# Sample rows taken eighth of nine in the output projection, and router logits from rows that are normalised only at the logits

## The reference

```python
def token_mixer(x, ...):
    z = rmsnorm(x, norm1_g) @ w_in           # q, kv, u, v, two gates
    attn = ...                               # latent attention, prompt or paged cache
    u = gelu(z_u); v = rmsnorm(gelu(z_v), sgu_norm_g)
    sgu = u * spatial_gate(v, w_s, b_s)      # mixes rows of one 128-row chunk
    merged = sigmoid(z_ga) * attn + sigmoid(z_gb) * sgu
    return x + merged @ w_o

def channel_mixer(x, ...):
    xt = rmsnorm(x, norm2_g)                 # x * rsqrt(mean(x*x) + eps) * norm2_g
    g_logit = xt @ w_rg + b_rg               # 8 groups, the best one is taken
    e_logit = xt @ w_re + b_re               # 64 experts, the best two of that group
    y = grouped_expert_ffn(xt, expert, weights, w_gate, w_up, w_down)
    return x + y
```

## Time and profile before

| | us |
|---|---|
| median of 3 runs | 2028.76 |
| lowest and highest run | 2025.43, 2029.05 |
| span of the profiled execution (first to last instruction) | 2028.6 |
| PE busy | 1864.8 (92%) |
| DVE busy | 600.3 (30%) |
| ACT busy | 426.1 (21%) |
| POOL busy | 300.7 (15%) |

### The profile page before, as it was taken

The page is one execution under the profiler, slowest core; times in us unless marked ns, Lnnn a source line. Parts: engine busy times, 40 slices in busy tenths (PEclk is TensorE's granted clock), DMA queues, the critical chain, the costliest instruction groups (busy, mean ns, idle before and its releaser), DMA issues. The chain is left out here.

```text
span 2028.6 us, 26767 instructions
## 1 busy us (share of the span) xinstructions
PE 1864.8 (92%) x10622; PEld 1093.4 (54%) x10622; DVE 600.3 (30%) x1385; ACT 426.1 (21%) x904; POOL 300.7 (15%) x428
## 2 busy tenths in 40 slices
PE   7999999999999999998999997999498888988884
PEld 5644444444445656565666664565365555655551
DVE  3110000022203334334455554565313211111116
ACT  3211111100003223322334443222111001110103
POOL 1021221111100000000111112244412111111100
PEclk9999999999999999988999998999599899998997
DMA  7212211378820000023999996344599999999986
GB/s 232 106 68 79 74 42 64 121 264 273 290 70 1 1 1 1 1 62 106 277 298 298 300 298 255 146 180 158 201 376 420 420 417 417 413 404 403 407 353 259
DMA packets 105267, 433.86 MB, mean 214 GB/s; under 512 B 24208, under 2 KB 29808, under 8 KB 74384
## 3 DMA queue, kind: packets, MB, share of 16 engines
q1 hardware_dynamic: 84880, 331.06, 43.3%
q0 software_dynamic: 20160, 101.24, 15.2%
q10 hardware_dynamic: 128, 0.20, 0.0%
HBM read 389.22 MB, written 63.66 MB: 223 GB/s over the span
## 5 line engine op out<-in xcount | busy, mean ns | idle before, releaser
L851 PE MATMUL psum<-arena 128*128 128x512 f32 (+1 forms) x1280 | 527.5, 567 | 0.0
L851 PEld LDWEIGHTS psum<-arena 128*128 128x128 f32 x1280 | 239.7, 190 | 259.9 <-issue 236.0
L1286 PE MATMUL psum<-arena 128*64 128x256 f32 (+1 forms) x2048 | 283.4, 410 | 64.6 <-DMA arena<-in_w_up_dram 64.5
L1286 PEld LDWEIGHTS psum<-arena 128*64 128x64 f32 (+1 forms) x2048 | 204.4, 155 | 133.8 <-issue 77.8
L1305 PE MATMUL psum<-arena 128*64 128x512 f32 (+1 forms) x512 | 131.5, 595 | 1.5 <-DVE arena L2243 0.9
L1916 DVE COPY arena<-psum 128x512 f32<-128x512 f32 (+5 forms) x52 | 27.8, 545 | 348.0 <-PE psum L896 194.0
L1046 PEld LDWEIGHTS psum<-arena 128*128 128x128 f32 x1024 | 112.7, 141 | 30.3 <-issue 27.4
L1046 PE MATMUL psum<-arena 128*128 128x128 f32 x1024 | 126.6, 276 | 1.2 <-DVE arena L1970 1.2
L1455 ACT ACTIVATE arena<-psum 128x512 f32<-128x512 f32 (+1 forms) x72 | 40.4, 562 | 411.5 <-PE psum L851 398.6
L1176 PE MATMUL psum<-arena 128*128 128x512 f32 x256 | 114.7, 606 | 1.3 <-ACT arena L1504 1.3
L2239 DVE TENSOR_TENSOR arena<-arena,psum 128x256 f32<-128x256 f32 x36 | 15.2, 421 | 318.6 <-ACT arena L1569 318.6
(11 more groups left out here) (307 smaller groups left out, 1956.4 us busy)
## 6 DMA issues: line engine op xcount, KB each, us to landing
arena<-in_w_gate_dram SPq DMA_DIRECT2D x64, 1024.0 KB, 13.1
arena<-in_w_up_dram SPq DMA_DIRECT2D x64, 1024.0 KB, 20.2
arena<-in_w_down_dram SPq DMA_DIRECT2D x64, 1024.0 KB, 21.6
arena<-in_w_in_dram SPq DMA_DIRECT2D x8, 2048.0 KB, 9.0
z_act<-arena SPq DMA_DIRECT2D x64, 256.0 KB
rope_turned<-arena SPq DMA_DIRECT2D x32, 512.0 KB
arena<-rope_turned SPq DMA_DIRECT2D x64, 256.0 KB
arena<-z_act SPq DMA_DIRECT2D x8, 2048.0 KB, 9.9
```

The source lines that it names most:

```text
L851: last = mm(out[:, 0:w], xn_t[:, k, t * P:t * P + P], w_blk[n % 2][:, k, 0:w], start=(k == 0), stop=(k == KD - 1))
L1286: last = mm(bank(2 + u)[rows, DE * x:DE * x + DE], xg_t[u][:, k, rows], w_e[slot][x][:, k, :], start=(k == 0), stop=(k == KD - 1))
```

## The change

Two things are changed, both in the output projection.

First, the order of the tiles is 0 to 6, 8, 7: a tuple `ORDER` gives the tile at each position, so that the 32 sample rows come at position 7 and the last 128 prompt rows at position 8. All buffers, products and stores follow.

Second, PE transposes the rows `x + merged @ w_o` as they are, not yet normalised, as soon as `add_x` has written them (`turn_x2` in place of `turn_normed`). The gains `norm2_g` are multiplied into the router's weights once, on POOL, before the cache attention (eight multiplies of 128x72; the gains come by a new DMA of 1024 single values early on SP's queue). DVE multiplies the logits by the reciprocal root of the row as it adds the bias. The normalised rows are still computed and stored for the experts. Since PE now reads `xr`, SP waits for that transpose (`ot_mm`) before it loads the next x into the same buffer.

```diff
+ORDER = tuple(range(NTP - 1)) + (NTP, NTP - 1)
...
+                sp.dma_start(g2_t, norm2_g[0].rearrange("(k p) -> p k", p=P)).then_inc(small_in, 16)
...
-            def z_load(t):
+            def z_load(n):
+                t = ORDER[n]
...
                 sp.wait_ge(o_n, n + 1)
                 sp.wait_ge(x2_cp, n + 1)
+                sp.wait_ge(ot_mm, n + 1)
                 x_again(n + 2)
                 sp.dma_start(xt_rows[n * P:n * P + P, :], normed_rows(n)).then_inc(xt_st[n % 2], 16)
...
             sp.wait_ge(at_ok, NT)
-            sp.wait_ge(ot_mm, 1)
...
-            def turn_normed(n, s, r=P):
-                pe.wait_ge(o_n, n + 1)
+            def turn_x2(n, r=P):
+                pe.wait_ge(x2_ok, n + 1)
                 pe.wait_ge(lg_ok, n + 1)
                 for k in range(KD):
-                    last = tr(bank(6, 2)[:, P * k:P * k + r], normed_rows(n)[0:r, P * k:P * k + P], ident[0:r, 0:r])
+                    last = tr(bank(6, 2)[:, P * k:P * k + r], xr[n % 2][0:r, P * k:P * k + P], ident[0:r, 0:r])
...
-            for n in range(1, NTP):
+            pe.wait_ge(wr_ok, 1)
+            for n in range(1, NT):
                 s = n % 2
-                mix(n + 1, 1 - s)
+                if n + 1 < NT:
+                    mix(n + 1, 1 - s)
...
-                turn_normed(n - 1, 1 - s)
-                out_product(n)
-                turn_merged(n + 1, 1 - s, rows_of(n + 1))
-                router(n - 1)
+                turn_x2(n - 1, rows_of(ORDER[n - 1]))
+                out_product(n, rows_of(ORDER[n]))
+                if n + 1 < NT:
+                    turn_merged(n + 1, 1 - s, rows_of(ORDER[n + 1]))
+                router(n - 1, rows_of(ORDER[n - 1]))
                 if n >= 2:
                     ranks(n - 2)
-            turn_normed(7, 1)
-            out_product(8, RS)
-            router(7)
-            ranks(6)
-            turn_normed(8, 0, RS)
-            router(8, RS)
+            turn_x2(8)
+            router(8)
             ranks(7)
...
-                if n == NTP:
-                    act.wait_ge(y_mm, NT)
+                if r == RS:
+                    act.wait_ge(y_mm, n + 1)
                     for g in range(4):
...
+                    last.then_inc(n_act, 1)
+                    merged_t(n + 1)
+                x2_stat(n, n % 2, r)
+                if r == P and n + 1 < NT:
+                    merged_t(n + 1, rows_of(ORDER[n + 1]))
+            normed_t(8)
             act.wait_ge(o_n, NT)
-            act.dma_start(xt_rows[NTP * P:TOK, :], xo[0][0:RS, :]).then_inc(xt_st[0], 16)
-            normed_t(8, RS)
+            act.dma_start(xt_rows[7 * P:8 * P, :], xo[0]).then_inc(xt_st[0], 16)
...
+            for k in range(KD):
+                last = G.tensor_scalar(w_router[:, k, :], w_router[:, k, :], g2_t[:, k:k + 1], None, ALU.mult)
+            last.then_inc(wr_ok, 1)
...
-                tt(lg_rows, bank(6)[0:r, 0:72], rbias[0:r, :], ALU.add).then_inc(lg_ok, 1)
+                stt(logits[0:r, t, :], bank(6)[0:r, 0:72], stat5[s][0:r, 3:4], rbias[0:r, :], ALU.mult, ALU.add).then_inc(lg_ok, 1)
```

More of the change, by code:

```diff
@@ L272, in build @@
         page_raw = take(NCH).bitcast(I32)
+        g2_t = take(KD)
         x2_at = [SIZE - NT * D]
@@ L680, in _, with x_again @@
                 sp.wait_ge(z_stored[u], 16 * (8 * NT // 2) + 16)
-            def z_load(t):
-                sp.dma_start(zt[t % 2][0:rows_of(t), :], z_act[t * P:t * P + rows_of(t), :]).then_inc(z_in[t % 2], 16)
-            def x_again(t):
-                sp.dma_start(xr[t % 2][0:rows_of(t), :], xp[t * P:t * P + P, :] if t < NTP else xs).then_inc(xr_in[t % 2], 16)
+            def z_load(n):
+                t = ORDER[n]
+                sp.dma_start(zt[n % 2][0:rows_of(t), :], z_act[t * P:t * P + rows_of(t), :]).then_inc(z_in[n % 2], 16)
+            def x_again(n):
+                t = ORDER[n]
+                sp.dma_start(xr[n % 2][0:rows_of(t), :], xp[t * P:t * P + P, :] if t < NTP else xs).then_inc(xr_in[n % 2], 16)
             for n in range(2, NCH):
@@ L1152, in mix @@
             def mix(n, s):
-                last_tile = isinstance(n, int) and n == NTP
-                r, wst = (RS, ws_ts) if last_tile else (P, ws_t)
+                r, wst = (RS, ws_ts) if ORDER[n] == NTP else (P, ws_t)
                 pe.wait_ge(v_n, n + 1)
@@ L1725, in _, with scatter @@
             ids_v = ids_sb.rearrange("p (n c) -> p n c", c=2)
-            def scatter(t):
-                pool.wait_ge(r_pos, t + 1)
+            def scatter(m):
+                pool.wait_ge(r_pos, m + 1)
+                t = ORDER[m]
                 for n in range(2 * t, 2 * t + 2):
@@ L1740, in _ @@
             for n in range(NT):
-                if n + 2 == NTP:
-                    pool.wait_ge(n_act, 4)
                 if n + 2 < NT:
-                    gate_attn(n % 2, attn[0:rows_of(n + 2), n + 2, :], n // 2 + 2, rows_of(n + 2))
-                keep_x2(n, n % 2, x2[0:rows_of(n), n, :], rows_of(n))
+                    t = ORDER[n + 2]
+                    if t == NTP:
+                        pool.wait_ge(n_act, 4)
+                    gate_attn(n % 2, attn[0:rows_of(t), t, :], n // 2 + 2, rows_of(t))
+                t = ORDER[n]
+                keep_x2(n, n % 2, x2[0:rows_of(t), t, :], rows_of(t))
                 if n >= 3:
@@ L2099, in wide, with choose @@
                 return x.unsqueeze(len(x.shape)).broadcast_to(list(x.shape) + [n])
-            def choose(t):
+            def choose(n):
+                t = ORDER[n]
                 lg = logits[:, t, :]
@@ L2147, in _ @@
             for n in range(1, NT):
-                u, r = n % 2, rows_of(n)
+                u, r = n % 2, rows_of(ORDER[n])
                 if n + 1 < NT:
-                    merge(n + 1, 1 - u, rows_of(n + 1), bs_t if n + 1 < NTP else bs_ts)
+                    t = ORDER[n + 1]
+                    merge(n + 1, 1 - u, rows_of(t), bs_t if t < NTP else bs_ts)
                 if n + 2 < NT:
-                    v_norm(n + 2, u, rows_of(n + 2))
+                    v_norm(n + 2, u, rows_of(ORDER[n + 2]))
                 add_x(n, u, n // 2 + 1, r)
-                take_logits(n - 1, logits[:, n - 1, :])
+                take_logits(n - 1)
                 norm2(n, u, n // 2, r)
@@ L2158, in _ @@
                 choose(n - 1)
-            take_logits(8, logits[0:RS, NTP, :], RS)
+            take_logits(8)
             stage_end(dve, 4)
```

46 lines of the change are left out of this document (24 added, 22 removed).

## The result

| | before | changed |
|---|---|---|
| median | 2028.76 us | 2033.46 us |
| runs, lowest and highest of the changed kernel | 11 | 11, 2031.58 to 2042.83 us |
| ratio of the times, 95% interval | | 1.0044 (1.003 to 1.0058) |
| profiled execution: time, span | span 2028.6 us | 2033.46, 2031.7 us |

The change makes the kernel slower, by little: 4.7 us by the medians, 6 to 12 us by the interval of the ratio. The two don't quite agree (the medians give 1.0023). One run of the kernel before took 3090.76 us and is left out of the ratio.

A forecast was written before the change was run, and what follows sets the result against it. PE was taken to lead up to the output projection's end, and DVE's choices for the last tile to start the expert stage behind it. 2.8 + 2.0 + 1.5 = +6.3 us gave 2035 us, range 2029.5 to 2038.5.

The forecast's parts named there:

- A: The end of DVE's last sum with x in the output projection; 1427.07 us before, forecast near 1432 to 1434.
- SP's new wait: In the full passes, later loads from `z_act` delay v_norm and the sum with x: +2.8 us.
- the pass-by-pass count: Delay carried through the full passes, less DVE's slack: 0.8, 0.8, 1.8, 1.8, then 2.8 us.
- The order: Before the last long product, the short product no longer covers DVE's merge of tile 7, so PE waits: +2.0 us.
- The clock: Around the last product, idle time lowers the granted clock: 0 to 2.95 us, plus 0.9 if transposes slow; 1.5 taken.
- The guess that the light work between the idle spells might hold the clock up: Before the last product, short pieces of PE work may prevent the fall, so about half the loss, 1.5 us, was taken.
- The rival built on it: Clock stays at 0.50 through the light stretch and the last product's first half: +8.7 us, 2037.4; chance 0.13.
- From A to the experts: From DVE's last sum to the expert stage, nothing added: 0, with a bound of +1 us for the slots' scatter.
- a shift of the last tile's choices shifts the whole expert stage by the same amount: Behind the output projection, early weights are already there, so DVE's last choices start the expert stage; delay passed on in full.
- The transposes of raw rows: Full passes gain nothing; at the end a 1.35 us wait goes, but DVE is late: 0, bounds -0.5 and 0.5.
- the first and third term: The forecast's parts for SP's new wait in the full passes, 2.8 us, and for the clock near the last product, 1.5.

The follow-up runs named there:

- the kernel with the loads: Changed kernel with DVE's merge first, tile 5's positions before the normed sample rows, and SP's loads ahead of its wait for the transposes; ratio 1.0011 to the kernel before.
- the last kernel: Kernel with the sample rows' router inside the last long product and GpSimd's drain removed, plus three unread products in PE's two waits; ratio 0.9993 to the kernel before.

## Why the prediction was right, point by point

The forecast was +6.3 us and the time 2035; it measured 2033.46. A moved by +6.8, the first expert product by +7.95, and the interval gives +6 to +12, so the median alone flatters the forecast: it is somewhat low. (A itself is at 1429.83 and not at 1432 to 1434, because the stage began 4.0 earlier in this trace.)

- *SP's new wait*, forecast 2.8, was 1.7. The issue 1.1 us behind the product's start and the lost slack of v_norm are as described, but the pass-by-pass count was too high: the load took 9.4 to 10.2 us from its issue to ACT's use in place of the 10.4 that was reckoned, and the load of one pass went out only 0.5 behind the product.
- *The order*, forecast 2.0, fits: it is what is left of 6.8 when 1.7 and 3.0 are taken off. It was not measured alone, since no kernel with this order and nothing else kept its clock. The merge of tile 7 began 9.0 behind the start of the sum of its pass (8.7 forecast), and TensorE stood 3.25 for it (about 3 forecast). Ahead of the last product it stood 0.99 (about 2 forecast), because the slow router filled more of that gap.
- *The clock*, forecast 1.5, was about 3.0. The last product lost 2.07; the start came at M + 7.26 in place of M + 6.3 (M is the end of the merge), and the 1.0 is the router at the lower clock, for whose logits VectorE waits. The guess that the light work between the idle spells might hold the clock up was wrong: it fell in all ten kernels with this order that left a gap open, and only a filling of both gaps kept it, up to A. With the rule cited from the Trainium skill (TensorE: Matmul & The Clock Gate, Part 1), that the low clock is the default and activity releases it, the trace agrees: 0.50 at 1408 to 1416, behind a stretch in which TensorE hardly worked. The rival built on it, 8.7 in all, set too large a price for the first half of the product, 2.95 where 2.07 were lost.
- *From A to the experts*, forecast unchanged. It holds up to the ranks (13.15 and 13.19), not beyond: 1.0 came on top, from GpSimd's drain by way of the clear that held VectorE's last conversion. The step "a shift of the last tile's choices shifts the whole expert stage by the same amount" had only VectorE's list in view. GpSimd's way to the table was as long.
- *The transposes of raw rows* gained nothing, as forecast. The reason given for the end of the stage was incomplete: taking away the wait of 1.35 brings the sample's product no nearer, since it also waits for the positions of tile 5, which end 0.20 ahead of it in the kernel before too. In the changed order the raw rows save a second wait on the norm (1.78 in the kernel with the order alone).

The errors of the first and third term, -1.1 and +1.5, nearly cancel. That the sum came out at A within 0.5 us is luck to that extent; the mechanisms are the ones forecast, their sizes are not.

## What to carry to other kernels

A short piece of work put ahead of a long one takes the cover from what the other engines do meanwhile; ask not how long it takes but what had been hidden under its neighbour. Where two chains reach a point at nearly the same time (here the ranks and the scatters), shortening one moves the bound to the other: measure at the point where they meet. And measure a stage from a point inside the trace, since the stages ahead of it differed by 12 us from execution to execution.

## What the hardware showed that was not expected

- The clock fell though TensorE never waited longer than 1.40 us between two groups ahead of the last product: in the kernel with the loads it was 0.62 in the stretch from 1404 to 1406. Three products of 0.95 us each, in the two gaps of the last kernel, kept it at 1.00 to the end of the product.
- GpSimd's drain behind indirect DMAs took 5.70 to 7.16 us in the ten traces that have it, counted from the end of its last scatter instruction.
- The conversion of 128x2 values on VectorE took 1.10 to 2.63 us in the nine kernels in which GpSimd's clear lay over it, and ended with the clear each time; in the other five it took 0.17. The longest, in the kernel with the loads:

```profile
1438.81 2.63 DVE L2140 CAST arena<-arena 128x2 uint32<-128x2 f32 x1
1439.55 1.87 POOL L1759 MEMSET arena<- 128x1024 f32 x2
```

  The Trainium skill (SBUF — State Buffer, section "SBUF: two separate sides") says that VectorE and GpSimd share a pair of ports under an exclusive lock. That fits the end of the row, 1441.44 and 1441.42; by the rows VectorE had started first, which the rule alone doesn't explain. In the kernel before the clear had started first.
